# Moving the ReLU of two feed-forward blocks from VectorE to ScalarE and its scaling to GpSimd, and packing a side job into consecutive units

## The reference

```python
x = x + squared_relu_mlp(rms_norm(x, ff_norm_g[i]), w_ff1[i], w_ff2[i])     # i = 0, 1

def squared_relu_mlp(h, w1, w2):       # w1: 1024 x 4096, w2: 4096 x 1024
    a = jax.nn.relu(h @ w1)
    return (a * a) @ w2

# second model: six vectors of 1024 from two conditioning inputs, for each layer
mod_x = silu_c @ ada_w[layer] + ada_b[layer]
mod_c = silu_cc @ ada_w[layer] + ada_b[layer]
```

## Time and profile before

| | us |
|---|---|
| three runs | 3733.01, 3738.42, 3752.55 |
| median | 3738.42 |
| time of the profiled execution | 3738.42 |
| its span in the trace | 3736.6 |
| PE busy | 3550.9 |
| DVE busy | 2034.4 |
| ACT busy | 1192.9 |
| POOL busy | 213.2 |

### The profile page before, as it was taken

One profiled execution on the slowest core, in us unless ns is written; L12 is line 12 of the kernel. 1 busy time (PEld: TensorE's weight loads), 2 busy tenths in 40 slices (PEclk: granted clock), 3 DMA queues, 4 the chain that ended last, 5 costly groups with the idle time before them and its releaser, 6 DMA issues.

```text
span 3736.6 us, 42196 instructions
## 1 busy us (share of the span) xinstructions
PE 3550.9 (95%) x17456; PEld 2809.5 (75%) x17456; DVE 2034.4 (54%) x3741; ACT 1192.9 (32%) x1993; POOL 213.2 (6%) x302
## 2 busy tenths in 40 slices
PE   7999999999989999999998989999998998879998
PEld 6657788887867788877985557888886885558886
DVE  5565688887555588873136664333335236654444
ACT  4353332234353332223112123332333212134332
POOL 0200000001130100010000001000001000000000
PEclk9999999999899999999998759999999998779999
DMA  4302244433112244434210011212122220113321
GB/s 165 112 16 79 79 158 152 153 116 104 55 35 79 79 158 158 153 119 144 66 53 20 23 48 46 68 57 68 57 68 85 98 68 18 40 45 94 98 92 66
DMA packets 214108, 317.01 MB, mean 85 GB/s; under 512 B 5304, under 2 KB 162618, under 8 KB 212636
## 3 DMA queue, kind: packets, MB, share of 16 engines
q1 hardware_dynamic: 198108, 243.00, 20.1%
q0 software_dynamic: 15808, 71.31, 5.6%
HBM read 300.66 MB, written 14.49 MB: 84 GB/s over the span
## 4 chain that ended last, share of the span: by engine, by line
PE 88%; DVE 7%; ACT 2%; issue 2%; DMA 1%; POOL 0%; SPq 0%; DVEq 0%; ACTq 0%; POOLq 0%
PE ps L94 87%; DVE t L115 3%; ACT t L100 2%; DVE t L107 2%; PE ps L97 1%; DVE t L111 0%; DVE t L112 0%; DVE ps L115 0%; DVE t L121 0%; DMA t<-gates_away 0%; DVE ps L107 0%; DVE t L118 0%; DVE t L125 0%; DMA t<-in_mem 0%; ACT L100 0%
## 5 line engine op out<-in xcount | busy, mean ns | idle before, releaser
L94 PE MATMUL ps<-t,t 128*128 128x512 f32 (+5 forms) x17040 | 3494.4, 369 | 159.0 <-DVE t L107 64.2
L94 PEld LDWEIGHTS ps<-t,t 128*128 128x128 f32 (+3 forms) x17040 | 2758.1, 192 | 868.7 <-issue 191.4
L100 ACT ACTIVATE t<-t 128x1024 fp32r<-128x1024 f32 (+4 forms) x1134 | 804.6, 746 | 1310.4 <-PE ps L94 910.3
L107 DVE TENSOR_TENSOR t<-t,t 128x1024 fp32r<-128x1024 f32 (+5 forms) x850 | 755.8, 918 | 590.7 <-ACT t L100 574.9
L100 ACT ACTIVATE t<-ps 128x512 f32<-128x512 f32 (+7 forms) x442 | 222.3, 529 | 833.4 <-PE ps L94 783.8
L115 DVE SCALAR_TENSOR_TENSOR t<-t,t,t 128x256 f32<-128x256 f32 (+3 forms) x927 | 437.6, 533 | 14.1 <-ACT t L100 7.3
L107 DVE TENSOR_TENSOR t<-ps,t 128x512 f32<-128x512 f32 (+4 forms) x293 | 188.5, 660 | 213.5 <-PE ps L94 146.4
L115 DVE SCALAR_TENSOR_TENSOR t<-ps,t,t 128x512 f32<-128x512 f32 (+1 forms) x228 | 139.8, 662 | 281.4 <-PE ps L94 261.3
L118 DVE COPY t<-ps 128x256 f32<-128x256 f32 (+3 forms) x162 | 73.0, 478 | 281.6 <-PE ps L94 262.9
L107 POOL TENSOR_TENSOR t<-t,t 128x64 f32<-128x64 f32 (+1 forms) x196 | 129.8, 688 | 1597.9 <-ACT t L100 1594.9
L100 ACT ACTIVATE t<-t,t 128x512 fp32r<-128x512 f32 (+3 forms) x160 | 96.1, 603 | 200.7 <-DVE t L107 127.8
(11 more groups left out here) (33 smaller groups left out, 296.0 us busy)
## 6 DMA issues: line engine op xcount, KB each, us to landing
t<-in_w_ff SPq DMA_DIRECT2D x64, 1024.0 KB, 5.4
t<-in_w_mlp SPq DMA_DIRECT2D x64, 1024.0 KB, 5.5
t<-in_ada_w POOLq DMA_DIRECT2D x48, 1024.0 KB, 5.8
t<-in_w_in SPq DMA_DIRECT2D x30, 1024.0 KB, 5.3
t<-in_w_qkv_o SPq DMA_DIRECT2D x12, 1024.0 KB, 5.1
t<-in_w_mem_kv SPq DMA_DIRECT2D x8, 1024.0 KB, 6.2
t<-in_w_mem_q SPq DMA_DIRECT2D x8, 1024.0 KB, 5.1
t<-in_w_mem_o SPq DMA_DIRECT2D x8, 1024.0 KB, 5.1
```

What stands on the lines that cost most here:

```text
L94: return Issued(self, self.e and self.e.matmul(o, l, r, start=start, stop=stop, skip_group_check=True))
L100: return Issued(self, self.e and self.e.activation(o, i, f, **kw))
L107: return Issued(self, self.e and self.e.tensor_tensor(o, a, b, op))
```

## The change

ReLU of a hidden tile is done by ACT from PSUM into TMP, without RS. POOL then multiplies TMP by RS in place. The square, the high part (ACT) and the low part (DVE) stay as they were. The conversions ahead, `convert(u.i + 2)`, are gone: block u.i + 1 is converted at the start of unit u, in ACT's order ahead of the ReLU of u, in DVE's order ahead of the low parts of u. The side job no longer skips units: its 24 steps start in the first 24 units of the block. POOL issues the DMA of a step between its multiplications.

```diff
-    mod_steps = [s for s in range(32) if s % 4 != 1 or s < 5 or s > 21][:24]
@@ tensor: modulate() (and the same renaming of b to s - 1 below)
-                if l is None or s - 1 not in mod_steps:
+                if l is None or s > 24 or s == 0:
                     return
-                b = mod_steps.index(s - 1)
-                pe.wait_ge("macc", l, b, 1)
+                pe.wait_ge("macc", l, s - 1, 1)
@@ scalar: up_late(j)
                 for u in f1[j]:
                     start(u)
+                    for x, t in enumerate(u.tiles):
+                        act.wait_ge(*ready(u, t))
+                        if tmp_free[x] is not None:
+                            act.wait_ge(*tmp_free[x])
+                        act.activation(TMP[x][:, :], t.views[0].ps, ACT.Relu).then_inc("ev", u.n, t.m, 0)
                     if u is f1[0][0]:
                         roots([((nkey, 0), P[6][:, :], 128, 0, ("sumsq", (nkey, 0), 7))], 1.0 / D)
-                    convert(u.i + 2)
                     for x, t in enumerate(u.tiles):
-                        act.wait_ge("ev", u.n, t.m, 0)
+                        act.wait_ge("scaled", key, j, t.m)
                         act.activation(TMP[x][:, :], TMP[x][:, :], ACT.Square).then_inc("sqr", key, j, t.m, 0)
...
+                        tmp_free[x] = ("hidden", key, j, t.m, 0)
@@ vector: modulate()
-                if l is not None and s - 1 in mod_steps:
+                if l is None or s > 24:
+                    return
+                if s > 0:
...
-                if l is not None and s in mod_steps:
+                if s < 24:
@@ vector: up(j)
-                    if l is not None:
-                        for x, t in enumerate(u.tiles):
-                            dve.wait_ge(*ready(u, t))
-                            dve.wait_ge("rs", (f"ff{l}", 0))
-                            if not first:
-                                dve.wait_ge("hidden", key, j if t.m > 1 else j - 1, (t.m + 2) % 4, 0)
-                            dve.scalar_tensor_tensor(TMP[x][:, :], t.views[0].ps, 0.0, RS[0][:, :], ALU.max, ALU.mult).then_inc(
-                                "ev", u.n, t.m, 0)
-                        convert(u.i + 2)
-                        if not first:
-                            modulate()
                     for t in u.tiles:
...                                                   # the low parts, as before
-                    if l is None:
+                    if not first:
                         modulate()
@@ vector: down units
                     add_to(u, streams, (lambda m, z: ("ev", f2[j - 1][b].n, m, z)) if j > 0 else None, gain)
-                    if l is not None and j < 7:
-                        convert(u.i + 2)
@@ gpsimd
             pl.wait_ge(*whole(U.mo[l][0]))
-            for b in range(24):
-                if b >= 2:
-                    pl.wait_ge("macc", l, b - 2, 1)
-                modulation_weights(b)
+            modulation_weights(0)
+            modulation_weights(1)
+            f1, f2 = U.ff[l]
+            key, b = "mix1" if l == 0 else "n1_0", 2
+            for j in range(-1, 8):
+                for u in f1[j + 1] if j < 7 else ():
+                    for x, t in enumerate(u.tiles):
+                        pl.wait_ge("rs", (f"ff{l}", 0))
+                        pl.wait_ge("ev", u.n, t.m, 0)
+                        pl.tensor_tensor(TMP[x][:, :], TMP[x][:, :], RS[0][:, :], ALU.mult).then_inc("scaled", key, j + 1, t.m)
+                    if b < 24:
+                        pl.wait_ge("macc", l, b - 2, 1)
+                        modulation_weights(b)
+                        b += 1
+                for u in f2[j] if j >= 0 else ():
+                    if b < 24:
+                        pl.wait_ge("macc", l, b - 2, 1)
+                        modulation_weights(b)
+                        b += 1
```

More of the change, by code:

```diff
@@ L708, in modulate @@
                     for c in range(2):
-                        ins = pe.matmul(P[7][:, 2 * m + c:2 * m + c + 1], tiles.ACC[b % 2][:, c, 128 * m:128 * m + 128],
+                        ins = pe.matmul(P[7][:, 2 * m + c:2 * m + c + 1], tiles.ACC[(s - 1) % 2][:, c, 128 * m:128 * m + 128],
                                         cst("ones", 128, 1), True, True)
-                ins.then_inc("mps", l, b)
-                free[7] = [("mod", l, b)]
+                ins.then_inc("mps", l, s - 1)
+                free[7] = [("mod", l, s - 1)]
             def up(j):
@@ L1417, in feed_forward @@
                         if l is not None:
-                            rs_free[0] = ("ev", f1[7][1].n, 3, 0)
+                            rs_free[0] = ("scaled", key, 7, 3)
                         for m in range(4 * b, 4 * b + 4):
@@ L1939, in modulate @@
                 step[0] += 1
-                if l is not None and s - 1 in mod_steps:
-                    b = mod_steps.index(s - 1)
-                    dve.wait_ge("mps", l, b)
+                if l is None or s > 24:
+                    return
+                if s > 0:
+                    dve.wait_ge("mps", l, s - 1)
                     for m in range(2):
-                        k = 2 * b + m
+                        k = 2 * (s - 1) + m
                         ins = dve.tensor_scalar(MOD[l][:, k, :], P[7][:, 2 * m:2 * m + 2], vec(f"ada_b{l}", k), None, ALU.add)
@@ L1948, in modulate @@
                         else:
-                            ins.then_inc("mod", l, b)
-                if l is not None and s in mod_steps:
-                    s = mod_steps.index(s)
+                            ins.then_inc("mod", l, s - 1)
+                if s < 24:
                     wv = tiles.ADA[s % 2][:, :].rearrange("p (k n) -> p k n", k=8)
```

## The result

| | before | after |
|---|---|---|
| median of 7 runs, us | 3733.22 (3730.31 to 3752.55) | 3764.69 (3746.36 to 3769.76) |
| profiled span, us | 3736.6 | 3768.6 |

The changed kernel takes 1.0067 times as long, with a 95% interval from 1.0052 to 1.0084: some 25 us slower by that ratio, 31 by the medians, and 32 by the two profiled spans. Forecast were 29, with 69% for slower by over 0.5%.

A forecast was written before the change was run, and what follows sets the result against it. PE was taken to bound the blocks without gaps, so only new waits count: 5 x 2.2 + 3.5 = 14.5 us a block, 29 for both, on 3738.4 gives 3767 us; range 3746 to 3790.

The forecast's parts named there:

- PE's pace and no slack to win: In both feed-forward blocks PE loses nothing today: 11.19 us a unit, 0.90 a step; only new waits count.
- The chain of a hidden tile: ReLU, POOL, ACT, DVE's low parts done at 4.7 us, then step and conversion: PE waits 1.0 us a group.
- Who gives way: At a group's second up unit POOL and DVE's conversion alternate: 1.7 us wait ahead of first down unit, 0.5 ahead of second.
- rival (a): In the blocks, engines don't hinder each other or POOL doesn't delay the conversion: 13 us in all, 3751 us; 20%.
- The sum: Five groups of 2.2 us plus 3.5 at the start: 14.5 us a block, 29 for both.
- the clash: POOL's multiplication meets DVE's conversion at a group's second up unit; with it a group loses 2.2 us instead of 1.0.
- Rival (e): PE's waits let the granted clock fall; under 1 of 20 us idle expected; given no case of its own.
- (b): POOL falls behind through its DMA's wait, multiplications fall into DVE's side job: 36 us on (a)'s 13, 3787 us; 12%.
- (c): Low parts come early enough, nothing changes: 3738 us; needs a chain of 3.7 us instead of 4.7; 10%.
- (d): Faster: relieved DVE reaches the last additions and norm earlier at the second block's end; at most 10 us, 3728; 3%.

The follow-up runs named there:

- the kernel with the conversions ahead: Changed kernel with convert(u.i + 2) put back on ACT and DVE: ratio to before 1.0059, blocks 404.3 us each.
- the doubled multiplication: Changed kernel with a second POOL multiplication per hidden tile, into a tile nobody reads: ratio to before 1.0337, blocks 457.8 and 457.7 us.
- kernel with scaling on DVE: Changed kernel with the multiplication by RS on DVE, ahead of the low parts, instead of POOL: ratio to before 0.9970, blocks 394.6 and 394.7 us.
- steps spread: Changed kernel with the side job's steps skipping units as before the change: ratio to before 1.0076, blocks 409.9 and 410.0 us.
- thirteen matmuls added: Kernel before with thirteen more matmuls behind its first feed-forward block, result unread: ratio to before 1.0001, blocks 389.3 and 389.2 us.

## Why the prediction was right

**PE's pace and no slack to win.** Right. In all kernels without waits the blocks take 389.2 or 389.3 us, whatever DVE, ACT and POOL do beside PE.

**The chain of a hidden tile.** Low parts at 4.7 us from the unit's end were forecast. PE ends a first up unit at 542.1 (ACT's pair of ReLUs starts 0.70 earlier, at 541.4), and the step starts at 546.6: 4.5. POOL's multiplication, priced by its additions, is 1.27 us (2.54 for two); 1.29 was taken.

**Who gives way.** Wrong: I had the two engines take turns, with half a conversion delayed by 1.3 us, so 1.7 us of wait ahead of the first down unit and 0.5 ahead of the second. The two instructions that matter, one by one, in the changed kernel:

```profile
554.08 1.22 DVE L107 TENSOR_TENSOR t<-t,t 128x1024 fp32r<-128x1024 f32 x1
554.28 2.17 POOL L107 TENSOR_TENSOR t<-t,t 128x512 f32<-128x512 f32 x1
```

The second half of the conversion starts at 554.08, and POOL is ready 0.2 us later, at 554.28. So the half takes its 1.22 us, and POOL's first multiplication takes 2.17 instead of 1.27. I had put POOL 0.1 us ahead of that half; the chain of the first up unit, 0.2 us shorter than forecast, turned the order round. The case against rival (a) names this outcome: POOL comes later and delays the low parts in place of the conversion. So the waits are 0.39 and 1.49. The Trainium skill (SBUF — State Buffer, "SBUF: two separate sides") says that whoever starts first holds the shared ports for the whole instruction. The trace agrees, with 2.17 us here and with 1.66 instead of 0.61 for DVE's small operations above. Turns are no rule either: in the kernel with the conversions ahead DVE's half, asked for at 607.88, took 3.48 us, since POOL's second multiplication went ahead of it as well.

**The sum.** 2.2 us a group were forecast, and 50.52 - 48.36 = 2.16 measured. That they agree so well is partly luck. The 2.2 were 1.0 for the chain and 1.2 for the clash. The clash measures 0.9 (POOL's pair, 3.42 instead of 2.54), the chain 1.0 (1.88 of waits without the 0.9), and 0.3 is what PE loses around its waits, which the sum didn't have. The step behind the second up unit starts 5.5 us after that unit's end where 5.9 were forecast. For a block 14.5 were forecast and 17.0 measured, of which two stretches at half the clock take 3.0 (37.85 and 37.94 instead of 36.40 in the second block), so 14.0. For the whole, 34 in the blocks less the 2 us of the start make 32 where 29 were forecast, so these errors partly cancel too.

**The term that was left out.** Rival (e), the clock, had got no chance: rows 11 showed 1.00 in windows with 0.5 and 2.8 us idle of 20. In the changed kernel it falls for 6.8 us in each block, and in a window where PE hardly waits:

```profile
620.00:670.00 50.00, 48.29 (x224) 39.41 (x222) 41.40 (x93) 15.19 (x20) 9.58 (x8) 1.00 0.50 165
670.00:680.00 10.00, 9.83 (x36) 7.88 (x37) 10.00 (x24) 0.00 (x0) 0.88 (x1) 0.83 0.56 190
```

It costs 6 of the 34 us. My windows of 20 us elsewhere were too few to exclude it. The kernels without waits, and the two with waits of at most 0.9 us, have none of it within the blocks; the doubled multiplication has eight times as much.

**The other rivals.** (a), no clash or none that counts, would have been 13 us; POOL's 3.42 us in each group answer it. The kernel with scaling on DVE, 11 us in the blocks, has no POOL to clash with but also a shorter chain, so it doesn't test (a). (b), POOL behind its DMA, doesn't happen in the changed kernel (0.93 us from 553.33, done as the tiles come), but does with the conversions ahead or the multiplication doubled. (c) and (d) would have been kernels as fast as before or faster; neither a chain of 3.7 us nor a gain at the end of a block shows.

## What to carry to other kernels

An engine with time to spare in the sum can still stop the one that bounds the kernel: ask for each of its instructions whether it is ready when its turn comes, and put work that is ready (here the side job) in front of work whose inputs still travel through other engines. Here moving an operation off DVE lengthened the chain that DVE waits for by two hand-overs and the slower engine's time. With the step put in that time it cost nothing, and it gained nothing either, since PE sets the pace of the blocks. And compare kernels by stages: here a change of 11 us in two stages was hidden by clock and moment elsewhere.

## What the runs showed of the hardware

- In the first block, waits of PE of up to 1.5 us, 12.1 us in all, came with 6.8 us at half the granted clock; waits of up to 1.2 us, 8.7 in all (conversions ahead), with 6.8 too; waits of up to 2.5 us, 40 in all (doubled multiplication), with 54.6; and waits of up to 0.9 us, 4.5 in all (scaling on DVE), with none.
- A stretch of 3.4 us at half the clock cost 1.5 us where PE had work without a wait, and nothing where PE would have waited for DVE behind it (a group of 50.2 us with and without, steps spread).
- Stretches at half clock in the stages outside the blocks differ between kernels: 17.1 to 61.4 us of them between the two blocks, with 440 to 457 us for that part of the program (453 with thirteen matmuls added).
- POOL takes 1.27 us for a product of two 128x512 fp32 tiles with DVE idle, and 2.17 when it starts 0.2 us behind a conversion's half of 1.22 us.
- A conversion's half on DVE that was asked for during the first of two multiplications of POOL took 3.48 us instead of 1.22: it waited for both.
